# Query tiles of a head in the order 7, 0, 6, 1, 5, 2, 4, 3

## What is computed

```python
s = jnp.einsum('bghqd,bgnd->bghqn', qb, kc) * scale          # 63 compressed keys
p_cmp = masked_softmax(s, cmp_end[None, :] <= t[:, None])
...
n_top = min(SLC_TOPN, n_slc)                                  # 16 of 16 blocks
p = masked_softmax(s, (pos <= t[:, None])[:, :, None])        # selected blocks
...
wmask = (kpos <= t) & (kpos > t - WINDOW) & (kpos >= 0)       # window of 512
...
return gb[..., 0:1] * o_cmp + gb[..., 1:2] * o_slc + gb[..., 2:3] * o_win
```

## Time and profile before

| | |
|---|---|
| median of 3 runs | 1433.62 us (1433.53 to 1433.7) |
| profiled execution | 1435.7 us, span 1433.9 us |
| TensorE matmuls busy | 1397.6 us, 97% |
| TensorE weight loads busy | 1209.4 us, 84% |
| VectorE busy | 872.7 us, 61% |
| ScalarE busy | 622.7 us, 43% |
| GpSimd busy | 174.6 us, 12% |
| mean granted TensorE clock | 0.996 of full |

### The profile page before, as it was taken

How to read it: one execution, slowest core, us unless ns; L and a number is a source line. 1 busy time by engine, 2 the same in 40 slices (tenths; PEclk the granted TensorE clock), 3 DMA queues, 4 the chain that set the end, 5 groups by cost and what they waited for, 6 DMA issues and landing times.

```text
span 1433.9 us, 21450 instructions
## 1 busy us (share of the span) xinstructions
PE 1397.6 (97%) x7790; PEld 1209.4 (84%) x7790; DVE 872.7 (61%) x1744; ACT 622.7 (43%) x1236; POOL 174.6 (12%) x192
## 2 busy tenths in 40 slices
PE   7999999999999999999999999999999999999999
PEld 7888888878999999999988878888888788888887
DVE  3002683007767777779783686666655697579764
ACT  5014303125555555551431468655555544444441
POOL 3433334520000000030242000000000000000000
PEclk9999999999999999999999999999999999999999
DMA  5212114200000000013010035444445946643332
GB/s 188 60 44 52 45 36 133 73 17 1 2 1 1 1 2 1 2 45 118 31 59 30 30 117 162 162 137 157 155 145 197 333 147 218 203 121 91 103 110 88
DMA packets 78253, 129.76 MB, mean 90 GB/s; under 512 B 8973, under 2 KB 26698, under 8 KB 78154
## 3 DMA queue, kind: packets, MB, share of 16 engines
q1 hardware_dynamic: 77968, 128.37, 28.1%
q10 hardware_dynamic: 186, 0.08, 0.0%
HBM read 94.87 MB, written 33.55 MB: 90 GB/s over the span
## 4 chain that ended last, share of the span: by engine, by line
PE 51%; DVE 3%; issue 1%; ACT 1%; DVEq 0%; ACTq 0%
PE ps L520 47%; PE ps L2134 2%; DVE hgrn_vg L1650 1%; PE ps L760 1%; DVE hgrn_k L1608 0%; PE ps L2182 0%; PE ps L2181 0%; PE ps L2204 0%; DVE x L1668 0%; DVE hT_low L773 0%; DVE hgrn_q L1607 0%; DVE hgrn_A L1616 0%; DVE hgrn_A L1583 0%; DVE rsqrt_a L586 0%; PE ps L2171 0%
## 5 line engine op out<-in xcount | busy, mean ns | idle before, releaser
L520 PE MATMUL ps<-mlp_w_high,hidden_high 128*128 128x512 f32 x448 | 174.3, 389 | 0.0
L520 PE MATMUL ps<-mlp_w_low,hidden_high 128*128 128x512 f32 x448 | 174.3, 389 | 0.0
L520 PE MATMUL ps<-mlp_w_high,hidden_low 128*128 128x512 f32 x448 | 174.3, 389 | 0.0
L520 PE MATMUL ps<-w_high,hT_high 128*128 128x512 f32 (+1 forms) x448 | 170.2, 380 | 0.7 <-ACT cmp_v L1083 0.7
L520 PE MATMUL ps<-w_low,hT_high 128*128 128x512 f32 (+1 forms) x448 | 168.2, 375 | 0.0
L520 PE MATMUL ps<-w_high,hT_low 128*128 128x512 f32 (+1 forms) x448 | 168.0, 375 | 0.0
L1309 ACT ACTIVATE mlp_w_high<-mlp_w_raw 128x512 fp32r<-128x512 f32 x112 | 70.6, 630 | 149.1 <-PE ps L520 149.1
L2114 PEld LDWEIGHTS ps<-nsa,probs_T 128*128 128x128 f32 x1056 | 133.2, 192 | 1.6
L1681 DVE TENSOR_TENSOR mlp_w_low<-mlp_w_raw,mlp_w_high 128x512 fp32r<-128x512 f32 x112 | 76.8, 690 | 92.0 <-ACT mlp_w_high L1210 92.0
L2114 PE MATMUL ps<-nsa,probs_T 128*128 128x64 f32 x1056 | 132.5, 269 | 0.0
L1761 DVE TENSOR_TENSOR mlp_w_low<-mlp_w_raw,mlp_w_high 128x512 fp32r<-128x512 f32 x112 | 77.1, 688 | 65.6 <-ACT mlp_w_high L1309 65.6
(11 more groups left out here) (233 smaller groups left out, 2811.9 us busy)
## 6 DMA issues: line engine op xcount, KB each, us to landing
hidden_raw<-hidden_pieces SPq DMA_DIRECT2D x112, 256.0 KB, 2.7
mlp_w_raw<-in_w_mlp_in_dram SPq DMA_DIRECT2D x32, 512.0 KB, 4.2
hidden_pieces<-hidden SPq DMA_DIRECT2D x64, 256.0 KB, 2.7
mlp_w_raw<-in_w_mlp_out_dram SPq DMA_DIRECT2D x64, 256.0 KB, 4.1
w_raw<-in_w_in_dram SPq DMA_DIRECT2D x56, 256.0 KB, 2.7
hidden_pieces<-hidden_s SPq DMA_DIRECT2D x48, 256.0 KB, 2.2
x_in<-in_x_dram SPq DMA_DIRECT2D x8, 512.0 KB, 7.2
w_raw<-in_w_out_dram SPq DMA_DIRECT2D x16, 256.0 KB, 2.6
```

Of the source, the lines that this page charges most:

```text
L520: ins = nc.tensor.matmul(out_ap, a_hl[i], b_hl[j], start=first and n == 0, stop=last and n == 2, skip_group_check=onto_a_sum_already_read)
```

## The change

The query tiles of each head are taken in the order 7, 0, 6, 1, 5, 2, 4, 3 in place of 0 to 7. Every other function is as it was, but all that hangs on an item's place in the list follows: the order on each engine, the score banks, which engine copies which group, and which items stand beside the query stack.

```diff
+TILE_ORDER = (7, 0, 6, 1, 5, 2, 4, 3)
+
+
 class Items:
...
             self.items.append(("cmp", hh, 0, []))
-            for t in range(NT):
+            for t in TILE_ORDER:
                 self.items.append(("slc", hh, t, list(range(t + 1))))
                 self.items.append(("win", hh, t, list(range(max(0, t - WIN_T), t + 1))))
```

## The result

| | before | changed |
|---|---|---|
| median of 4 runs | 1433.57 us (1432.8 to 1433.7) | 1454.8 us (1453.31 to 1456.68) |
| ratio | | 1.0141, 95% interval 1.0126 to 1.0157 |
| profiled execution, span | 1435.7, 1433.9 us | 1455.0, 1453.2 us |
| first 512- or 256-column score to the next stage's first matmul | 325.60 to 622.94: 297.3 us | 327.46 to 642.28: 314.8 us |
| from there to the end of the span | 811.0 us | 810.9 us |

The change makes the kernel slower by 21.2 us. In the profiled executions the difference is 19.3: 17.5 lie inside the attention, nothing behind it, and 1.9 ahead of it, where no instruction was moved. The start of the attention lay between 324.99 and 327.46 us in the fourteen profiled kernels of this case, so those 1.9 us are not put down to the change.

What follows compares the result with a forecast made beforehand. TensorE was taken to bound the attention, with waits on ScalarE and VectorE. New waits less old gave +16.4 us, a second layout +11; +13 was taken on 1433.6, so 1446.6 us, own range 1439 to 1453, whole range 1433 to 1459.

Steps and rivals of the forecast that it cites:

- the clock, a rival at 0.17: Odd heads' 2.04 us waits each lower TensorE's granted clock: 4 x 1.7 = 6.8 us more, 1453; chance 0.17.
- A: Tile 7's window scores, heads 1 to 7, wait for its selected item's exponential on shared banks: 12.2 us.
- B: Tile 6's window transposes start late because the copy of its selected probabilities isn't done: 3.4 us over eight heads.
- C: Query stack halves, now after tiles 5 and 2, delay tiles 3 and 4; with leftovers, 16.5 us over heads 0 to 6.
- D: Attention's start: TensorE idles 3.1 us for the first exponential, 0.65 more at the fifth score, less 1.64: +2.1 us.
- E: All old TensorE waits of the eight heads go: 17.8 us less.
- The first road: Sum of new waits in the attention less the old ones: 12.2 + 3.4 + 16.5 + 2.1 - 17.8 = +16.4 us.
- The second road: TensorE's work laid end to end at free pace with the new waits: heads of 38.0 and 38.9 us, stage +11 us.
- the half microsecond a head: Old head laid out at free pace comes to 36.7 us, half a microsecond short; +11 us if it goes, 16 if it stays.
- Faster: Rival: small pairs let VectorE and ScalarE catch up, so B and C vanish: -3.5 us, 1424 to 1430; chance 0.13.

Runs made afterwards that it cites:

- the kernel with the exponential first: Changed kernel, with ScalarE issuing the exponential of tile 7's selected item ahead of the copy of the item before the compressed one: 1444.45 us.
- small tiles first: Tile order 0, 1, 7, 2, 6, 3, 5, 4 in place of the changed kernel's order: 1439.69 us, ratio 1.0026 to the kernel before.
- only tile 7 moved: Tile order 7, 0, 1, 2, 3, 4, 5, 6 in place of the changed kernel's order: 1474.97 us, ratio 1.028 to the kernel before.
- both edits: Changed kernel, with tile 7's exponential ahead of ScalarE's copy and VectorE's finalize ahead of the query stack's subtraction: 1434.89 us, ratio 1.0005.

## Why the prediction was right, and where it wasn't

The forecast was 1446.6 us, its own range to 1453 and the whole range to 1459; measured were 1454.8. Direction and the mechanism of the waits held, and the clock, a rival at 0.17, came true. The time is 8.2 us over the forecast and above its own range; the whole range holds it only because it had room for that rival.

**A, tile 7's window scores.** Right. Predicted 4 x 2.04 + 3 x 1.35 = 12.2 us, measured 4 x 1.87 + 3 x 1.21 = 11.1. The alternation between heads, its cause in ScalarE's list and the shared banks are as stated. Issuing the exponential first took the difference away.

**B, tile 6's window transposes.** Right in kind, too large. Predicted 0.34 and 0.52 us; they start 0.31 late against the free pace in every head, 2.5 us and not 3.4. Most of it doesn't show as an idle time in brackets (0.15 in one row), since the transposes before it overlap.

**C, the query stack.** All three places are right: 0.56 idle before tile 3's scores, which is 0.81 against the free pace if counted from start to start as in the earlier trace rows (0.84 predicted), 0.45 at tile 4's fifth transpose (0.55 to 0.60), and 0.86, or 1.03 against the free pace, before tile 4's window transposes in even heads (1.21). That makes 3 x 1.26 + 4 x 2.29 = 12.9 us where 16.5 were predicted: the leftovers of 0.1 to 0.3 a place weren't there, and small errors of the layout all went one way. VectorE waited for the query stack 14 times for 22.9 us, 1.6 each (about 1.5 predicted).

**D, the start.** 3.05 us measured, 3.1 predicted. The 0.65 at the fifth score isn't in the trace, so D is 3.05 - 1.64 = 1.4 us where 2.1 were predicted. The shorter drop at the start gives back up to 1.7, the estimate above, so that the new start may have cost next to nothing.

**E and the sum.** The first road had 16.4 us, the second 11, and the forecast took 13 between them. Measured are 11.0 to 12.7. That is near the forecast partly by luck. The terms that the trace places come to 11.1 + 2.5 + 12.9 + 1.4 - 17.8 = 10.1, so A to D were 6.3 too large together. This is the first road with its terms put right, and it is 0.9 to 2.6 us short; those have no place of their own in the trace. The second road's 11 had the same terms in it, and with them put right it falls to about 5. So the half microsecond a head that its layout couldn't place stayed, and taking a value below the first road was right for another reason, the size of A to D. Heads were predicted at 38.2 and 39.2 us and are 37.7 and 39.6, mean 38.65 and not 38.7.

**The clock.** This step failed: "I assume the drop at the start stays as it is and no new one comes." Both halves of it failed: the drop at the start was half as long, and drops came in three of four odd heads. The rival had named the place, the length and the mark by which to tell ("under about 1.5 us there is no drop": 1.21 brought none, in three heads here and in all seven of the kernel with the exponential first). Its chance was too low. The evidence for it was a drop behind 2.04 us of idleness and one behind 1.64; against it stood that the first is one case and that there had been gaps before the second, and this got 0.17 against 0.60. Its price was low as well: 6.5 us for three drops is 2.2 each, not 1.7, because the one of head 3 ran on for some seven microseconds. With the stage's 17.5 us in place of 13 the sum is 1433.6 + 17.5 = 1451, and the rest to 1454.8 is the later start of the stage, 1.9, and that the profiled execution of before lay 2.1 us above its median, the one of the changed kernel 0.2. The Trainium skill ("TensorE: Matmul & The Clock Gate", section "Why this matters for your kernels") warns of idle gaps longer than those of the heads; by it no drop would have come there. The traces go against it.

**Faster.** Its mark was "if they wait under 0.3 us and tile 4's transposes not at all"; they waited 0.56 and 0.45. The small pair between two large ones gave VectorE little: it waited 27.4 us for the query stack before and 22.9 with the change. Moving an instruction on VectorE itself took it to 14.7, in the kernel before.

## What to carry to other kernels

Before the order of the work is changed, look at what stands queued behind each waiting instruction on an engine with a fixed order: an independent 0.9 us of finalize moved ahead of a wait gained 11.8 us here, where reordering the tiles cost 21.2. Large work behind a special item inherits that item's constraints; here it met shared banks and a copy, two things that the sizes of the tiles don't tell. And price a new wait at the clock too, if the trace of before has a drop after a wait of about that length: the same wait counted 1.87 us by itself and about 4 with its drop.

## What was not expected of the hardware

- After a wait of 1.87 us TensorE's clock fell in six of eight cases, in other heads each time, and after 1.21 us in none of 33 in six traces, nor after the 1.25 of the small tiles first, in none of 14. The kernel with only tile 7 moved fits between them (1.93: two of three; 1.55: none of four). The length of the wait alone doesn't decide: the 1.64 us at the start were followed by a drop in all six kernels that have them. In the next stage TensorE idled 2.04 us for VectorE in each of the fourteen kernels, and the clock fell behind it in ten, so in the kernel before, but stayed at 1.00 with both edits, in windows of that kernel around its wait before 632.75:

```profile
632.00:635.00 3.00, 2.25 (x20) 2.29 (x21) 3.00 (x4) 0.79 (x2) 1.47 (x7) 1.00 0.01 3
635.00:638.00 3.00, 3.00 (x29) 3.00 (x29) 2.34 (x3) 0.00 (x0) 0.00 (x0) 1.00 0.02 5
```

- With only tile 7 moved, one drop lasted about 24 us while TensorE had no idle time in the record, where those of the changed kernel lasted 3 to 7. What keeps it down is open.
- The drop at the start of the attention was shorter after the longer wait: 3.4 us in seven of the eight kernels that idle 3.05 us there (6.8 in one), 6.8 us or more in all six that idle 1.64. Why is open.
- Ten transposes put into a wait held the clock as matmuls did: 1447.66 and 1447.89 us.
